# Second block's decay and beta projection: weights held still in four column groups, tokens streamed, and a turn by ten small products

## What is computed

```python
aq, ak, av, dq, dk, dv, dz, da, db, ga, gd = split_cols(h @ w_in)
...
def dn_inputs(pq, pk, pv, pa, pb):
    qkv = centred_short_conv(jnp.concatenate([pq, pk, pv], axis=-1), conv_w)
    ...
    beta = jax.nn.sigmoid(pb.reshape(pb.shape[0], T, N_DIR, DN_HEADS))
    g = -jnp.exp(a_log) * jax.nn.softplus(pa.reshape(pa.shape[0], T, N_DIR, DN_HEADS) + dt_bias)
    return q_d, k_d, v_d, g, beta
```

## Time and profile before

| | us |
|---|---|
| median of 3 runs | 3776.81 |
| the three runs | 3767.11, 3776.81, 3777.61 |
| span of the profiled execution | 3778.2 |
| PE busy in it | 3606.1 (95%) |
| DVE busy | 1848.7 (49%) |
| ACT busy | 1185.7 (31%) |
| small projection and mask on PE | 1703.05 to 1736.22 |

### The profile page before, as it was taken

How to read it: one execution, slowest core, us unless ns; L and a number is a source line. 1 busy time by engine, 2 the same in 40 slices (tenths; PEclk the granted TensorE clock), 3 DMA queues, 4 the chain that set the end, 5 groups by cost and what they waited for, 6 DMA issues and landing times. The chain is left out here.

```text
span 3778.2 us, 46616 instructions
## 1 busy us (share of the span) xinstructions
PE 3606.1 (95%) x18410; PEld 2808.8 (74%) x18410; DVE 1848.7 (49%) x3350; ACT 1185.7 (31%) x2093; POOL 702.7 (19%) x532
## 2 busy tenths in 40 slices
PE   7999999999999999999988988988999999999998
PEld 6756778888888888876557878646788468888886
DVE  4276992223685554244468884469321142232322
ACT  3155771222311211132434553128311032211210
POOL 1162000010101111010020110119201213333333
PEclk9999999999999999998998996999999999999999
DMA  3100111112233222113011212200122111111111
GB/s 131 38 2 25 42 39 56 53 56 78 89 95 109 92 90 95 51 60 123 1 22 33 46 34 72 78 17 2 26 73 64 56 54 47 45 56 45 45 56 45
DMA packets 266342, 211.67 MB, mean 56 GB/s; under 512 B 65680, under 2 KB 231184, under 8 KB 265744
## 3 DMA queue, kind: packets, MB, share of 16 engines
q1 hardware_dynamic: 264368, 201.61, 17.3%
q10 hardware_dynamic: 1760, 7.08, 0.9%
HBM read 185.33 MB, written 21.50 MB: 55 GB/s over the span
## 5 line engine op out<-in xcount | busy, mean ns | idle before, releaser
L95 PE MATMUL ps<-halves 128*128 128x512 f32 x10408 | 2408.2, 392 | 18.8 <-DVE halves L1542 6.6
L95 PEld LDWEIGHTS ps<-halves 128*128 128x128 f32 x10408 | 1957.1, 188 | 441.4 <-issue 26.9
L95 PE MATMUL ps<-arena 128*128 128x512 f32 (+2 forms) x1040 | 397.1, 540 | 11.6 <-issue 6.0
L95 PEld LDWEIGHTS ps<-arena 128*128 128x128 f32 x1040 | 199.4, 213 | 172.4 <-issue 160.3
L1521 POOL TENSOR_TENSOR tmps<-tmps 128x512 f32<-128x512 f32 x128 | 143.5, 1121 | 981.4 <-ACT tmps L1489 981.4
L1542 DVE TENSOR_TENSOR halves<-tmps,halves 128x512 fp32r<-128x512 f32 x128 | 89.0, 698 | 433.4 <-ACT halves L1497 433.4
L1425 ACT ACTIVATE halves<-raws 128x2048 fp32r<-128x2048 f32 x62 | 118.4, 1910 | 554.7 <-PE ps L95 532.5
L1528 POOL TENSOR_TENSOR arena<-arena 128x512 f32<-128x512 f32 x128 | 164.7, 1294 | 191.4 <-DVE arena L1569 191.4
L1489 ACT ACTIVATE tmps<-ps 128x512 f32<-128x512 f32 x128 | 76.6, 598 | 364.0 <-PE ps L95 354.0
L1569 DVE TENSOR_TENSOR arena<-ps,arena 128x512 f32<-128x512 f32 x128 | 87.7, 690 | 194.6 <-PE ps L95 188.5
L1365 DVE SCALAR_TENSOR_TENSOR arena<-arena,sc 128x128 f32<-128x128 f32 x448 | 163.4, 365 | 15.9
(11 more groups left out here) (300 smaller groups left out, 3548.7 us busy)
## 6 DMA issues: line engine op xcount, KB each, us to landing
raws<-in_w_ff SPq DMA_DIRECT2D x31, 1024.0 KB, 6.5
raws<-in_w_mlp SPq DMA_DIRECT2D x31, 1024.0 KB, 5.3
mixw<-in_w_in SPq DMA_DIRECT2D x56, 512.0 KB, 4.0
arena<-in_w_ada SPq DMA_DIRECT2D x48, 512.0 KB, 3.9
arena<-in_w_in SPq DMA_DIRECT2D x5, 2048.0 KB, 8.8
arena<-in_x SPq DMA_DIRECT2D x8, 1024.0 KB, 8.2
h_stash<-arena SPq DMA_DIRECT2D x1, 5120.0 KB, 20.6
inverses<-arena ACTq DMA_DIRECT2D x20, 256.0 KB, 2.9
```

The source lines that it names most:

```text
L95: ins = e.matmul(out_ap, l, r, start=i == 0, stop=i == n - 1)
```

## The change

The small projection is done the other way round: the weights (128 features by 32 columns) are held still and the tokens stream, in three pieces of 512, 512 and 256. Slice `k` of the eight goes to output partitions `32 * (k % 4)`, so that four column groups of the array each sum two of the eight slices. ACT copies the three pieces to a new buffer `ABQ` (128 partitions: four partial sums of 32 features). Ten products of `ABQ` (as the tile held still) with `SEL`, four identities of 32 stacked, then add the four partial sums and turn them to tokens in one go; they stand in round 1 of the convolutions, and the mask's product with them. `SEL` is made by one reduction on DVE from the identity. ACT's and DVE's logarithms move behind round 1, and the strip `dvv` waits for the third piece in place of the tenth tile.

```diff
-            "dvv": (0, w2[:, 1792:2304], 8, 512, ("ab", 9)),
+            "dvv": (0, w2[:, 1792:2304], 8, 512, ("ab", 2)),
...
         def tensor_ab(e):
             e.wait_ge(*bk.clear(("n2", 4, 6)))
             e.wait_ge(*bk.clear(("n2", 4, 7)))
+            w = strip_view("ab")
+            for p, (n0, N) in enumerate(PIECES):
+                key = ("ab", p)
+                o = bk.open(key, b_ea)
+                e.wait_ge(*bk.vacant(key))
+                e.wait_ge(*strip_there("ab"))
+                for k in range(8):
+                    c = 32 * (k % 4)
+                    ins = e.matmul(o[c:c + 32, 0:N], w[:, k, :], hrhs(k, n0, N), start=k < 4, stop=k >= 4)
+                ins.then_inc(*bk.filling(key))
+
+        def tensor_ab_turned(e):
+            key = ("abt",)
+            o = bk.open(key, b_ea)
+            e.wait_ge(*bk.vacant(key))
+            e.wait_ge(*bk.clear(("ab", 2)))
+            e.wait_ge(*b_1.at(1))
             for t in range(10):
-                tensor_tm(e, "ab", ("ab", t), t, 32, b_ea)
+                ins = e.matmul(o[:, t * 32:t * 32 + 32], ABQ[:, t * 128:t * 128 + 128], SEL, start=True, stop=True)
+            ins.then_inc(*bk.filling(key))
             o = bk.open(("mask",), b_ea)
...
         def scalar_ab(e):
+            for p, (n0, N) in enumerate(PIECES):
+                key = ("ab", p)
+                e.wait_ge(*bk.full(key))
+                e.activation(ABQ[:, n0:n0 + N], bk.tile(key)[:, 0:N], ACT.Copy).then_inc(*bk.emptying(key))
+
+        def scalar_ab_logs(e):
             e.wait_ge(*z_x.at(8))
-            for t in range(10):
-                key = ("ab", t)
-                e.wait_ge(*bk.full(key))
-                e.activation(AB[:, t, :], bk.tile(key)[:, 0:32], ACT.Copy).then_inc(*bk.emptying(key))
+            key = ("abt",)
+            e.wait_ge(*bk.full(key))
+            e.activation(AB, bk.tile(key)[:, 0:320].rearrange("p (t c) -> p t c", c=32),
+                         ACT.Copy).then_inc(*bk.emptying(key))
...
+        def vector_ab_select(e):
+            e.wait_ge(*z_x.at(8))
+            e.tensor_reduce(SEL, ident[:, :].rearrange("p (c j) -> p j c", c=4), AX.X, ALU.add).then_inc(*b_1.tick())
...
         (tensor_conv, after the pieces of round i)
+                if i == 1:
+                    tensor_ab_turned(e)
...
         (scalar_conv, ahead of round i)
+                if i == 2:
+                    scalar_ab_logs(e)
...
         (vector_conv, ahead of round j)
+                if j == 2:
+                    vector_ab(e)
...
-            vector_ab(e)
+            vector_ab_select(e)
             vector_conv(e)
```

More of the change, by code:

```diff
@@ L1705, in build @@
         b_ea = C("ab_emptied_act")
-        b_1, b_2, b_ab = C("ab_biased"), C("ab_log"), C("ab_done")
+        ABQ, SEL = R(F0 + 24592, 1280), R(CB + 2848, 32)
+        b_1, b_2, b_ab = C("ab_selection_biased"), C("ab_log"), C("ab_done")
         d_one = C("ones")
@@ L1730, in scalar_ab @@
             e.activation(rw[:, 16:32], rw[:, 16:32], ACT.Exp).then_inc(*av.tick())
-            e.wait_ge(*b_1.at(2))
+            e.wait_ge(*b_1.at(3))
             e.activation(tg1, AB, ACT.Abs).then_inc(*av.tick())
@@ L1736, in scalar_ab @@
             e.activation(tg1, tg1, ACT.Ln, bias=1.0).then_inc(*b_2.tick())
+        def vector_ab_select(e):
+            e.wait_ge(*z_x.at(8))
+            e.tensor_reduce(SEL, ident[:, :].rearrange("p (c j) -> p j c", c=4), AX.X, ALU.add).then_inc(*b_1.tick())
         def vector_ab(e):
             e.wait_ge(*l_rw.at(1))
-            e.wait_ge(*bk.clear(("ab", 9)))
+            e.wait_ge(*bk.clear(("abt",)))
             e.tensor_tensor(ga3, ga3, bc(rw[:, 0:16].unsqueeze(1), [P, 10, 16]), ALU.add).then_inc(*b_1.tick())
             e.tensor_scalar(be3, be3, -1.0, None, ALU.mult).then_inc(*b_1.tick())
-            e.wait_ge(*b_1.at(2))
+            e.wait_ge(*b_1.at(3))
             e.tensor_scalar(tg2, AB, 0.0, None, ALU.max).then_inc(*dv.tick())
```

## The result

| | before | after |
|---|---|---|
| median of 6 runs, us | 3765.51 | 3741.32 |
| the six | 3757.99 to 3777.61 | 3733.37 to 3751.22 |
| span of the profiled execution | 3778.2 | 3731.6 |
| PE busy in it | 3606.1 | 3562.2 |

The ratio is 0.992, 95% interval 0.9902 to 0.9939: faster by 0.8%, or 24.2 us. The two profiled executions lie 46.6 us apart, nearly twice that. Where these 46.6 us are is the first thing to read, and only part of them belongs to the change.

What follows compares the result with a forecast made beforehand. PE, busy without a gap through this stage, was taken as the bound: 33.17 + 1.33 - 4.4 - 2.1 - 0.4 = 27.6 us gained. Span 3778.2 less 27.6 and 1.4 gave 3749.2 us, range 3740 to 3758.

Steps and rivals of the forecast that it cites:

- Small projection and mask, 33.17 us removed: Ahead of the convolutions: the 80 old products and the mask leave PE's path, saving 33.17 us.
- Half clock into round 0, 1.33: Convolution rounds 0 and 1: with PE no longer at 1.2 GHz at round 0's start, 1.33 us more saved.
- Streamed projection, 4.4 of 4.4 to 17.2: New small projection: 4.4 us added if four column groups overlap fully, 17.2 with no overlap.
- Turn 2.1, mask 0.4: Convolution round 1: ten turning products add 2.1 us at full clock, the mask's product 0.4.
- The logarithms and PE's waits, cost nought: Convolutions: moved logarithms and waits for the turn cost PE nothing, with some 3 us of cover.
- The sum, 27.6: Norm and convolution stage on PE: savings less added work give 27.6 us gained.
- The delta rule, "3 us either way": From round 9 on: the chain moves as a whole; clock changes on other products allowed 3 us either way.
- From the span to the median: Whole kernel: span 3778.2 less 27.6, and the three-run median 1.4 below the span, give 3749.2 us.
- Two at a time: Streamed projection: four groups do no better than two, 8.6 us, time 3753.5; chance 0.12.
- No overlap: Streamed projection: groups run one after another, 17.2 us at full clock, time 3762; chance 0.04.
- its fall of the clock: Streamed projection without overlap: clock also falls 1.7 us in, 32.7 us, time 3779; chance 0.03.
- The logarithms in the way: Mid-convolutions: ACT and DVE chain overruns its cover, PE stands 3 to 10 us, 3752 to 3760; chance 0.06, other waits included.

Runs made afterwards that it cites:

- one_group: The changed kernel with all eight slices of the small projection summed in one column group; 3750.93 us, ratio 0.9948 to the kernel before.
- neighbours: The changed kernel with the two products of each column group placed one behind the other; 3738.22 us, one run.
- again: The changed kernel once more, unaltered; 3745.38 us, ratio 0.9924 to the kernel before.
- before_again: The kernel before, unaltered, for a second profile; 3782.39 us, one run.
- spread: The kernel before with its ten old tiles moved, two to each of rounds 1 to 5, and logarithms in round 6; 3810.02 us, ratio 1.009.
- spread2: As spread, but ACT copies each pair in the same round, right behind the round's pieces; 3761.57 us, ratio 0.9966 to the kernel before.
- warm_more: The changed kernel plus unread products: last two delta-rule steps, fourteen in every step, twelve in the norm's wait; projection pieces 0, 2 earlier; 3740.67 us, ratio 0.9909.
- combined: As warm_more, but without the fourteen unread products in every delta-rule step; 3727.5 us, ratio 0.9898 to the kernel before.

## Why the prediction was right or wrong

The mechanism was right: every term of the 27.6 us came out within 0.2 us. The step that failed is the size of the clock's swing outside the stage. The prediction allowed "3 us either way" for it and took the one profiled execution and the median of three runs as the level; the runs showed a delta rule of 446.0 and 462.1 us in the same kernel, and a median of before 11.3 us below the one taken.

**Small projection and mask, 33.17 us removed: right.** They are gone from PE's path and nothing took their place.

**Half clock into round 0, 1.33: right.** Rounds 0 and 1 took 24.15 against 24.07.

**Streamed projection, 4.4 of 4.4 to 17.2: right,** 4.44, and 17.28 in one_group is the other end. Two groups give 8.72, the number of the rival. The Trainium skill (TensorE: Matmul & The Clock Gate, Part 3, "Measured speedup vs the span model") would have made it 5.6 by four row groups (1.2 less in the sum, where the prediction wrote 1.3); this kernel's four column groups give 3.89 times. Its rule of strict order (same part, "What overlaps and what doesn't") does not describe neighbours, where products behind a waiting one start with it: 4.49 us in place of 8.6.

**Turn 2.1, mask 0.4: right,** 2.15 and 0.52, the mask 0.1 over.

**The logarithms and PE's waits, cost nought: right.** ACT's chain ended at 1746.5 with no wait on PE, and the cover, put at "some 3 us", measures 3.7. The turn's identity is one short reduction on DVE behind the last norm, as put, and the transfers ran under rounds 0 and 1 without a mark on PE.

**The sum, 27.6: right.** The stage gained 27.5 in the profiled executions; again's is the same 171.9, before_again's 197.8 against 199.4, as it spends 3.4 us less at half clock.

**The delta rule, "3 us either way": wrong.** This term was too small by several times. The stage differs by 16 us between two executions of the same changed kernel, and by 7 between two of before. The prediction saw the clock of 0.86 and drew the right consequence, that its changes "will fall on other products", but sized it as if they moved a little; one step alone is 11.5 us longer when it falls to the half clock. The work ahead of the change, for which the prediction had no term at all, swings by 8.0 us as well (1694.6 to 1702.6).

**From the span to the median: wrong.** Forecast: 3778.2 - 27.6 - 1.4 = 3749.2. The 3778.2 and the three runs' median of 3776.81 both lay high, which is chance and no fault of the mechanism: over six runs before is 3765.5, over the 41 beside the experiments 3772.7. So the time of 3741.3 is 7.9 below the forecast: the median of before is 11.3 lower than taken, and the gain 3.4 less than 27.6. The measured time is only 1.3 above the lower end of the range, and that end had been laid by the lowest of the three runs. A forecast from the middle of the runs' spread, given that one of three lay 9.7 lower, would have been some us lower, though no row showed the six-run median.

**The rivals.** Two at a time: refuted by 4.44 us, its price confirmed by 8.72. No overlap: refuted, and so is its fall of the clock, by one_group at 1.00 for 17.3 us. The logarithms in the way: refuted as the kernel stands, true once they take 3.7 us more.

**What stays open.** Whether the change also shortens the delta rule. Six profiled executions with the streamed projection and nothing else altered later have 446.0, 462.1, 449.7, 448.6, 447.8 and 457.0; four with the old form of the product (before twice, spread, spread2) have 461.3, 468.2, 466.3 and 463.7. Only again, of the six, reaches the four, and most of the difference is in the last two steps: 85 us in each of the four, 71 to 77 in five of the six. So the rival of the first two expectations, that the changed kernel has a shorter delta rule, is not refuted; again shows only that it does not have it every time. On the whole times the gains beyond the stage's own share are -2.5 us (24.2 less 26.7, the mean of before's two stages less 171.9), +3.2 (again) and +10.9 (one_group: 24.4 less 13.5); for spread2 and spread, which keep the old products, the same sum gives +2.8 and -2.7. That leans to some us of gain beyond the stage's 27, and the runs don't settle it: it would take several profiled executions of each kernel. What makes the clock fall at one execution's step and not at another's isn't shown either.

## What to carry to other kernels

A product of few columns pays for loading its tokens as the held tile: turned round, weights held in four column groups and tokens streamed, it costs a quarter of the stream, and a turn by a stack of identities adds the partial sums for 0.106 us a record. Read the clock beside such a stage: here 17 of the 27.5 us were time at 1.2 GHz that the old products brought on themselves and their neighbours, and moving them among long streams kept it up only in part. When forecasting an absolute time, take the spread of the runs before as a term of its own, and look for a stage whose clock swings before trusting the one profiled execution. A filler meant for a wait has to stand ahead of the semaphore that PE waits for; the fourteen that stood behind it cost their own time.

## What the runs showed of the hardware

- Four column groups in fp32 with 512-column streams: 4.44 us, two 8.72, one 17.28. About 0.1 us is lost against full overlap, and interleaving the groups or placing each one's products together is the same (4.44 and 4.49).
- The clock stayed at 1.00 for 17.3 us with only one of four column groups in use, but fell within a pair of tiles of 32-column products standing between pieces of 512 (0.83 in that stretch, 0.50 in the next). PE is busy in both; in the second, the loads are too (3.10 of 3.10 us against 5.20 of 17.30).
- In the delta rule, where PE waits about 60 us of 450, one program is at 1.2 GHz for 85 us in one execution and for 123 in the next, and the stage is 16 us longer. A stop of 4.4 us in a stage without gaps was followed by a clock of 0.57 for 3.6 us. Products that fill waits did not force it up: 16.4 us at 1.2 GHz in the last step of warm_more, none in that of combined, with the same fillers ahead of its joins.
